# First section of a transformer trunk: weights by fourths on one queue, half blocks of x on another, both blocks per fourth

## The reference

```python
def swiglu_ffn(x, w_in, w_out):
    gate, up = jnp.split(x @ w_in, 2, axis=-1)
    return (jax.nn.silu(gate) * up) @ w_out
...
    for l in range(DEPTH):
        h = layer_norm(ALPHA * h + 0.5 * swiglu_ffn(h, ffn_w_in[l, 0], ffn_w_out[l, 0]), ...)
        h = layer_norm(ALPHA * h + hybrid_mixer(h, w_in[l], w_o[l], ...), ...)
        h = layer_norm(ALPHA * h + 0.5 * swiglu_ffn(h, ffn_w_in[l, 1], ffn_w_out[l, 1]), ...)
```

## Time and profile before

| what | value |
|---|---|
| median of 3 runs | 971.4 us (971.05 to 971.62) |
| profiled execution, its own time | 971.12 us |
| its span in the profile | 969.2 us |
| TensorE busy (matmul) | 958.2 us, 99% of the span |
| VectorE busy | 660.9 us |
| ScalarE busy | 508.7 us |
| GpSimd busy | 29.1 us |
| mean traffic of the DMA engines | 186 GB/s |

### The profile page before, as it was taken

One profiled execution on the slowest core, in us unless ns is written; L12 is line 12 of the kernel. 1 busy time (PEld: TensorE's weight loads), 2 busy tenths in 40 slices (PEclk: granted clock), 3 DMA queues, 4 the chain that ended last, 5 costly groups with the idle time before them and its releaser, 6 DMA issues.

```text
span 969.2 us, 14472 instructions
## 1 busy us (share of the span) xinstructions
PE 958.2 (99%) x5135; PEld 806.7 (83%) x5135; DVE 660.9 (68%) x966; ACT 508.7 (52%) x688; POOL 29.1 (3%) x27
## 2 busy tenths in 40 slices
PE   8999999999999999999999999999999999999997
PEld 5888888888877888888888888888888788888886
DVE  5655656689998565655676565657999876566555
ACT  5554455445774545545455455545457655454541
POOL 0000000010002000000010000002000010000000
PEclk9999999999999999999999999999999999999999
DMA  9656566565324655557555655565643355555551
GB/s 313 236 173 216 173 201 230 189 217 175 131 88 160 230 174 198 192 177 243 171 189 174 215 175 194 194 219 183 234 161 111 121 199 177 192 197 174 197 193 43
DMA packets 123873, 180.04 MB, mean 186 GB/s; under 512 B 5824, under 2 KB 98112, under 8 KB 123072
## 3 DMA queue, kind: packets, MB, share of 16 engines
q1 hardware_dynamic: 123552, 178.91, 54.7%
q0 software_dynamic: 144, 0.62, 0.2%
q10 hardware_dynamic: 144, 0.07, 0.0%
HBM read 178.52 MB, written 1.05 MB: 185 GB/s over the span
## 4 chain that ended last, share of the span: by engine, by line
PE 98%; DVE 1%; DMA 1%; SPq 0%; issue 0%; ACT 0%; DVEq 0%
PE bank L535 30%; PE bank L539 16%; PE ybank L501 10%; PE ybank L507 10%; PE ybank L505 10%; PE bank L428 3%; PE bank L474 2%; PE bank L481 2%; PE bank L477 2%; PE ybank L474 2%; PE ybank L481 2%; PE ybank L477 2%; PE bank L660 1%; PE bank L727 1%; PE ybank L739 1%; PE ybank L744 1%
## 5 line engine op out<-in xcount | busy, mean ns | idle before, releaser
L1105 DVE TENSOR_TENSOR w_lo<-raw,w_hi 128x2048 fp32r<-128x2048 f32 (+1 forms) x155 | 355.1, 2291 | 238.5 <-ACT w_hi L879 238.5
L535 PE MATMUL bank<-xT,w_hi 128*128 128x512 f32 x1280 | 446.4, 392 | 0.0
L879 ACT ACTIVATE w_hi<-raw 128x2048 fp32r<-128x2048 f32 x160 | 305.7, 1911 | 251.9 <-PE bank L539 112.1
L539 PE MATMUL bank<-xT,w_lo 128*128 128x256 f32 x1280 | 359.5, 281 | 0.0
L535 PEld LDWEIGHTS bank<-xT,w_hi 128*128 128x128 f32 x1280 | 240.2, 188 | 52.7
L539 PEld LDWEIGHTS bank<-xT,w_lo 128*128 128x128 f32 x1280 | 240.8, 188 | 1.6
L501 PE MATMUL ybank<-w_hi,yT_hi 128*128 128x512 f32 x416 | 165.9, 399 | 0.3
L507 PE MATMUL ybank<-w_hi,yT_lo 128*128 128x512 f32 x416 | 162.9, 391 | 0.0
L505 PE MATMUL ybank<-w_lo,yT_hi 128*128 128x512 f32 x416 | 162.0, 389 | 0.0
L501 PEld LDWEIGHTS ybank<-w_hi,yT_hi 128*128 128x128 f32 x416 | 78.2, 188 | 18.2 <-issue 2.6
L507 PEld LDWEIGHTS ybank<-w_hi,yT_lo 128*128 128x128 f32 x416 | 77.9, 187 | 18.4
(11 more groups left out here) (127 smaller groups left out, 806.0 us busy)
## 6 DMA issues: line engine op xcount, KB each, us to landing
raw<-in_ffn_in SPq DMA_DIRECT2D x172, 512.0 KB, 4.5
raw<-in_ffn_out SPq DMA_DIRECT2D x88, 512.0 KB, 3.9
raw<-in_w_in SPq DMA_DIRECT2D x40, 512.0 KB, 4.4
raw<-in_w_o SPq DMA_DIRECT2D x16, 512.0 KB, 4.0
gb<-in_ln_gb SPq DMA_DIRECT2D x6, 1024.0 KB, 7.2
raw<-in_w_in SPq DMA_DIRECT2D x4, 520.0 KB, 6.6
raw<-in_ffn_in SPq DMA_DIRECT2D x8, 256.0 KB, 5.6
xn<-in_x SPq DMA_DIRECT2D x4, 256.0 KB, 4.3
```

The costliest lines, as they stand in the source:

```text
L535: m = eng.matmul(dst[:, :], wh[:, k, g, cols], xT[:, kk, :, :].rearrange("p a n -> p (a n)"), start=kk == 0, stop=False, skip_group_check= ...
L539: m = eng.matmul(dst[:, SEQ:2 * SEQ], wl[:, k, g, cols], xT_hi[:, kk, :], start=False, stop=kk == KT - 1, skip_group_check=True)
L879: eng.activation(w_hi[:, s, 0:width], raw[:, s, 0:width], ACT.Copy).then_inc(hi_done, 1)
L1105: eng.tensor_tensor(w_lo[:, s, 0:width], raw[:, s, 0:width], w_hi[:, s, 0:width].bitcast(F32), ALU.subtract).then_inc(lo_done, 1)
```

## The change

x reaches the chip by two queues: ScalarE issues the first halves of both blocks right after the unit matrix, SyncE the second halves, after unit 0's four fourths. SyncE issues unit 0's fourths first of all, and unit 2 by fourths too. `xn_ready` is no longer awaited for these transposes, but `x_loaded` itself. TensorE transposes the first half of both blocks, runs three more products of zeros, and then takes each fourth with both blocks. The transposes of the second halves stand before and within unit 0's last fourth, into `bank[2]` and `bank[3]`, one per block. ScalarE and VectorE follow that order; both SiLUs and both gated products now come one after the other, before unit 3. `unit_used` begins at 3 instead of 2, because no transpose frees a unit any more.

```diff
-            return (l * (UNITS // RING) + u_static // RING + c + 1 - (u_static % RING < 2)) * 32
+            return (l * (UNITS // RING) + u_static // RING + c) * 32
...
+                else:
+                    load_ffn_in(l, w, b + 3, b + 3, 1, 1)
+                    load_ffn_out(l, w, b + 4, b + 4, 0)
+                with eng.Fori(1 if l + w > 0 else 2, NCH) as c:
...
+            def load_piece(u, k):
...
+                half, chunk = u % 2, u // 2
+                eng.dma_start(dst, src[:, 4 * half + k, :, chunk * CHUNK:(chunk + 1) * CHUNK])\
+                   .then_inc(piece_loaded[4 * u + k], 16)
...
+            for k in range(4):
+                load_piece(0, k)
+            load_x(0, 1)
+            load_x(1, 1)
+            for u in (1, 2):
                 for k in range(4):
...
-            load_x(0)
-            load_pieces(0)
-            load_x(1)
-            load_pieces(1)
+                    load_piece(u, k)
...
+            def zero_products(n):
...
+                for i in range(n):
+                    m = eng.matmul(ybank[i % 4][:, :], zeros[:, 0:P], zeros[:, 0:BANK], start=True, stop=True)
...
+            def first_T(t, h):
...
+                if h > 0:
+                    eng.wait_ge(xT_ready, t + 1)
+                eng.wait_ge(x_loaded[2 * t + h], 16)
+                transposes(bank[2 + t], [xn[:, t, (4 * h + k) * P:(4 * h + k + 1) * P] for k in range(4)])\
+                    .then_inc(xT_psum, 1)
...
+            def first_pieces():
...
+                first_T(0, 0)
+                first_T(1, 0)
+                zero_products(3)
+                piece(0, 0, 0)
+                piece(0, 0, 1)
+                piece(0, 1, 0)
+                piece(0, 1, 1)
+                piece(0, 2, 0)
+                piece(0, 2, 1)
+                first_T(0, 1)
+                piece(0, 3, 0)
+                first_T(1, 1)
+                piece(0, 3, 1).then_inc(unit_used, 1)
                 for k in range(4):
...
+                    for t in range(T):
+                        m = piece(1, k, t)
+                        if k == 3:
+                            m.then_inc(gu_done, 1)
...
-            eng.sem_inc(unit_used, RING - 1)
...
+            eng.sem_inc(unit_used, RING)
...
-                stage_hi(l, 2 * w, (0,))
                 if first:
-                    pieces_hi(0)
+                    for u in range(2):
+                        first_hi(0, u)
+                        first_hi(1, u)
+                        piece_hi_part(u, 0)
...
+                    for k in range(4):
+                        piece_hi_part(2, k)
+                    silu(l, f, 0, 0, 0)
+                    silu(l, f, 0, 1, 0)
+                    split_hi(l, b, 3)
...
             eng.dma_start(cst[:, 0:EARLY], consts[:, 0:EARLY]).then_inc(cst_loaded, 16)
+            for t in range(T):
+                eng.dma_start(xn[:, t, 0:BANK], x[t * P:(t + 1) * P, 0:BANK]).then_inc(x_loaded[2 * t], 16)
             eng.wait_ge(pool_setup, 1)
...
                 if l == w == 0:
-                    stage_lo(l, 0, 0)
-                    pieces_lo(0)
-                    stage_lo(l, 0, 1)
-                    pieces_lo(1)
...
+                    for u in range(2):
+                        first_lo(0, u)
+                        first_lo(1, u)
+                        piece_lo_part(u, 0)
...
+                    gated(l, f, 0, 0, 0)
+                    gated(l, f, 0, 1, 0)
+                    split_lo(l, b, 3)
...
-            eng.wait_ge(raw_loaded[2], 32)
+            eng.wait_ge(piece_loaded[11], 16)
```

More of the change, by code:

```diff
@@ L276, in trunk @@
         x_loaded = [sem(f"x_loaded{n}") for n in range(T * HALVES)]
-        piece_loaded = [sem(f"piece_loaded{n}") for n in range(8)]
+        piece_loaded = [sem(f"piece_loaded{n}") for n in range(12)]
         piece_hi = sem("piece_hi")
@@ L548, in wait_piece @@
                     eng.wait_ge(whole, u + 1 + first)
-            def pieces(u, t):
-                tok = slice(t * P, (t + 1) * P)
-                for k in range(4):
[L555 to L573, removed]
+            def first_T(t, h):
[4 more added lines that the diff above has]
+                    .then_inc(xT_psum, 1)
@@ L879, in split_hi, with piece_hi_part, first_hi @@
                 eng.activation(w_hi[:, s, 0:width], raw[:, s, 0:width], ACT.Copy).then_inc(hi_done, 1)
[L881 to L887, removed]
+            def piece_hi_part(u, k):
+                cols = slice(k * BANK, (k + 1) * BANK)
+                eng.wait_ge(piece_loaded[4 * u + k], 16)
+                eng.activation(w_hi[:, u, cols], raw[:, u, cols], ACT.Copy).then_inc(piece_hi if k < 3 else hi_done, 1)
+            def first_hi(t, h):
+                eng.wait_ge(xT_psum, 2 * h + t + 1)
+                eng.activation(xT_hi[:, 4 * h:4 * h + 4, t * P:(t + 1) * P],
+                               bank[2 + t][:, :].rearrange("p (k n) -> p k n", k=4), ACT.Copy).then_inc(xT_hi_done, 1)
             def stage_hi(l, j, tiles):
@@ L1106, in split_lo, with piece_lo_part, first_lo @@
                                   ALU.subtract).then_inc(lo_done, 1)
[L1108 to L1117, removed]
+            def piece_lo_part(u, k):
+                cols = slice(k * BANK, (k + 1) * BANK)
+                if k < 3:
+                    eng.wait_ge(piece_hi, 3 * u + k + 1)
+                else:
+                    eng.wait_ge(hi_done, u + 1)
+                eng.tensor_tensor(w_lo[:, u, cols], raw[:, u, cols], w_hi[:, u, cols].bitcast(F32), ALU.subtract)\
+                   .then_inc(piece_lo if k < 3 else lo_done, 1)
+            def first_lo(t, h):
+                eng.wait_ge(xT_hi_done, 2 * h + t + 1)
+                part = (slice(None), slice(4 * h, 4 * h + 4), slice(t * P, (t + 1) * P))
+                eng.tensor_tensor(xT_lo[part], bank[2 + t][:, :].rearrange("p (k n) -> p k n", k=4),
+                                  xT_hi[part].bitcast(F32), ALU.subtract).then_inc(xT_ready, 1)
             def stage_lo(l, j, t):
@@ L1203, in ffn @@
                 if l == w == 0:
-                    stage_lo(l, 0, 0)
-                    pieces_lo(0)
-                    stage_lo(l, 0, 1)
-                    pieces_lo(1)
-                split_lo(l, b, 2)
-                gated(l, f, 0, 0, 0)
-                split_lo(l, b, 3)
-                gated(l, f, 0, 1, 0)
+                    for u in range(2):
+                        first_lo(0, u)
+                        first_lo(1, u)
+                        piece_lo_part(u, 0)
+                        piece_lo_part(u, 1)
+                        piece_lo_part(u, 2)
+                        piece_lo_part(u, 3)
+                    for k in range(4):
+                        piece_lo_part(2, k)
+                    gated(l, f, 0, 0, 0)
+                    gated(l, f, 0, 1, 0)
+                    split_lo(l, b, 3)
+                else:
+                    split_lo(l, b, 2)
+                    gated(l, f, 0, 0, 0)
+                    split_lo(l, b, 3)
+                    gated(l, f, 0, 1, 0)
                 split_lo(l, b, 4)
```

44 lines of the change are left out of this document (25 added, 19 removed).

## The result

The changed kernel takes 972.91 us (median of 20 runs, 972.06 to 973.84), the kernel before 971.38 us (20 runs). The ratio is 1.0015, 95% interval 1.0008 to 1.0021: it is slower by 1.5 us, which is under the 0.2% bound of the prediction.

A forecast was written before the change was run, and what follows sets the result against it. TensorE, busy 958.2 of 969.2 us, bounds the kernel. First product at 8.0 plus a 13.2 us section puts unit 2 at 21.2 against 21.07; 971.3 plus 0.3 for the median gives 971.6 us, range 970.2 to 973.1.

The forecast's parts named there:

- rival (3): Start: weights hold up x, so block 1's first half lands late; at 7.1 us the loss is 1.4 us, 972.8; chance 0.15.
- the prediction's own sign: Forecast wrong if first product before 7.2 or after 9.3 us, the forecast wait is missing, or products stand 0.43 us apart.
- Where the time is decided: Whatever moves unit 2's first product, before at 21.07 us, moves the end equally, if nothing later becomes late.
- The section: First product to unit 2's first: products 11.0, slow first three 0.28, transposes 1.0, added wait 0.95; 13.2 us against 14.04.
- The landing of block 1's first half: Third transfer on ScalarE's queue, sharing with weights: lands at 5.8 us, between ends of 4.8 and 7.1; break-even 5.6.
- The step: Landing estimate: packets alternate one to one, 0.98 MB at 290 GB/s from 2.0 us, seen 0.4 us later.
- the high end of the prediction: Latest landing of block 1's first half: both queues move equal bytes, 1.18 MB by 6.0 us, seen 1.1 later: 7.1.
- From landing to first product: Start: 0.3 us to first transpose, 0.64 to ScalarE, 0.49 to the split, 0.63 for it, 0.15 to TensorE: 2.2 us.
- The zero products: Three after the first transposes, 1.3 us at most, hidden in TensorE's wait for the split: cost nothing.
- a rival of 0.04: TensorE's clock stays low for the first 24 products, 0.2 us more each, 4.8 in all: 976.4; chance 0.04.
- Other edits: Cost nothing: unit 2's low half 0.8 us ahead, unit 3 with 1.1 us of cover, unit 4's later load harmless.
- fourth rival: Low clock after the idle start, 976.4; chance 0.04, since granted clock read 1.00 despite 1.58 us idle at 5.45.

The follow-up runs named there:

- e4: Changed kernel with both second-half transposes together, ahead of block 0's products of unit 0's last fourth; 972.37 us.
- e2: Changed kernel without the three zero products between the first transposes and the first product; 974.20 us.
- e3: Changed kernel with five more zero products right after the first seven, ahead of the transposes; 972.44 us.
- e8: Changed kernel with unit 2 loaded and split whole, as before, instead of by fourths; 972.63 us.
- e9: Changed kernel with x's second halves moved ahead of the weights on SyncE's queue, first halves still on ScalarE's; 973.01 us.
- e1: Changed kernel with all x on SyncE's queue, both blocks' first halves ahead of unit 0's fourths; 970.86 us.
- e5: Kernel before with only block 0's two x halves moved to ScalarE's queue, SyncE starting with unit 0's fourths; 973.91 us.
- e7: Changed kernel with x first on SyncE's queue and both second-half transposes together; 970.16 us.

## Why the prediction was right, and where its steps were not

The forecast was no change beyond 0.2%, 971.6 us in a range of 970.2 to 973.1. The measured 972.91 lies in it, near the upper end, and is rival (3), which had a chance of 0.15: the change loses what its later start costs. By the prediction's own sign, a first product after 9.3 us, its mechanism was wrong: the first product came at 9.86. That the time still lay within the range is partly luck. The start was 1.9 us later than forecast, the section 0.2 us longer, and unit 2 came at 23.30 instead of 21.2 us. The profiled execution, 973.20 us, is outside the range.

- **Where the time is decided: right.** The rest after unit 2's first product was the same to 0.03 us.
- **The section, 13.2 us: 13.44 measured.** The wait for the high half of unit 1's first fourth was 0.76 us by the starts (16.45 to 17.44, less 0.23), 0.59 of it idle, for 0.7 forecast, and e4 shows that the order of the transposes makes it.
- **The landing of block 1's first half, 5.8 us forecast: 7.4 measured.** This is the term that was mis-sized, and it is most of the miss. Three parts of it were off. The step took packets one to one, so that 0.98 MB had to move; the changed kernel's trace shows equal bytes by 6.5 us (0.59 and 0.58 MB), 1.17 MB, as the high end of the prediction had it. At the step's 290 GB/s, 0.2 MB more are 0.7 us. These bytes had moved at 6.5 us and not at 6.0 (2.0 plus 1.17 MB at 290 GB/s), 0.5 us more: from 2 to 4 us the rates were 109 and 184 GB/s. And the half was seen 0.9 us later, not 0.4. The high end was 7.1; this execution was later still; in e2, e3, e4 and e8, with the same order of transfers, the half landed at 7.0 to 7.1. e9 separates the parts: with the rates restored the bytes had moved by 5.9 us, but the half still landed at 7.0. So the second queue makes the landing late, and the rates add nothing that shows. Why the last bytes are seen so much later there stays open. e1 shows that the landing is the cause of the loss: 2.0 us back.
- **From landing to first product, 2.2 us: 2.4 measured.** The transposes took 1.1 instead of 0.6 us, which the forecast had not in it; the step from landing to first transpose was 0.3 shorter.
- **The zero products: wrong.** They were costed at nothing with no gain, and the clock was a rival of 0.04. Their cover was as good as gone: they ended at 9.71 us, and the product came at 9.86. e2 is 1.3 us worse without them, and e3 won 0.5 us by pace, so the clock is at work in this very stretch. Without the three the time would have been 974.2 us, outside the range.
- **Other edits: right.** Unit 2's low half came 1.0 us ahead for 0.8 forecast, unit 3's ended at 28.0 us (two of 2.29 from 25.72), 1.2 ahead of its use at 29.2, for 1.1 forecast, and unit 4's load was issued at 20.0 us without a wait of TensorE. e8 confirms it for unit 2.

The sum of before and after: the start cost 2.83 us (9.86 less 7.03), the section gave 0.60, and the span grew by 2.2. The medians differ by 1.5 us, since the two profiled executions lie on opposite sides of theirs. The prediction's errors on the landing and on the pace of the transposes both lie in the start.

## What to carry to other kernels

When a first product waits for one small tensor, put that tensor first on one queue, ahead of everything large; a second queue does not carry it past the first, it makes it wait for as much of the other's traffic. Count for each idle stretch in front of the first products what it does to TensorE's clock as well. Cheap products in it were worth 1.3 us here (e2), though they did not give the fast pace every time (e9). In a hand-written order, check what an in-order engine holds between the last producer and the next consumer: moving one block of four transposes by three products was worth 0.6 us.

## What the runs showed of the hardware that was not expected

- A start with two queues, weights in 1 KB rows on one and x on the other, moved 109 and 184 GB/s in the third and fourth microsecond; before, one queue with x first 272 and 314, two queues with x on both 258 and 292. Why the first accesses to the weights are slow stays open; no run here takes it apart.
- Two queues with work moved equal bytes, not equal packets: 0.59 MB in 610 packets and 0.58 MB in 421 by 6.5 us in the changed kernel. From 2 to 3 us, where ScalarE's queue carried the unit matrix, the packets were about equal (114 and 99 in the earlier trace rows), and the prediction took its share from there.
- In e2 the granted clock fell from 1.00 to 0.50 at 7.7 to 7.8 us, as the transposes ended and the gap of 1.3 us began, and stayed low over 12 products; the gap of 1.58 us in the earlier trace rows did no harm. What stood before differed: there, 1.04 us of transposes right behind the zero products; here, two short groups with 1.13 and 0.71 us of idle time before them.
- The granted-clock column reads 1.00 in stretches whose pace shows the low level: in e5 the products from 9.46 us on were 0.43 us apart, and the column said

```profile
9.46:14.27 4.81, 4.81 (x11) 3.71 (x12) 2.46 (x5) 1.41 (x3) 0.00 (x0) 1.00 1.09 379
```

  so near the start of an execution the distance of two products is the surer sign. The prediction's fourth rival leaned on that column for the gap at 5.45 us; there the distance of 0.23 us from 8.00 us on bears it out. The pace also differs between executions that have the same work up to there: the eight transposes took 1.91 us in e1 and 1.20 us in e7. That may be what spreads the runs of e9 (971.57 to 974.25, against 969.81 to 970.57 in e7); only one execution of each was profiled.
